# Hybrid trunk step (HGRN2, attention, Hyena, 16 experts): ring order of two modulation units, and an eighth place for expert weights in layer 1

## The reference

```python
a = jnp.einsum('td,edf->etf', t, w_gate)      # 16 experts, 1024 -> 512
b = jnp.einsum('td,edf->etf', t, w_up)
hid = jax.nn.silu(a) * b * gates.T[:, :, None]
out = jnp.einsum('etf,efd->td', hid, w_down)  # 512 -> 1024
```

## Time and profile before

| | |
|---|---|
| median of 3 runs | 874.86 us (872.3 to 875.55) |
| profiled execution | 872.13 us, its span 869.9 us |
| TensorE busy | 820.4 us, 94% |
| VectorE, ScalarE, GpSimd busy | 33%, 20%, 4% |
| DMA, mean | 336 GB/s over the span, 292.53 MB |
| expert stage of layer 0 | about 239 to 465 us |
| expert stage of layer 1 | about 633 to 861 us |

### The profile page before, as it was taken

One profiled execution on the slowest core, in us unless ns is written; L12 is line 12 of the kernel. 1 busy time (PEld: TensorE's weight loads), 2 busy tenths in 40 slices (PEclk: granted clock), 3 DMA queues, 4 the chain that ended last, 5 costly groups with the idle time before them and its releaser, 6 DMA issues.

```text
span 869.9 us, 13266 instructions
## 1 busy us (share of the span) xinstructions
PE 820.4 (94%) x5760; PEld 514.4 (59%) x5760; DVE 284.2 (33%) x587; ACT 176.4 (20%) x308; POOL 37.9 (4%) x67
## 2 busy tenths in 40 slices
PE   4999999799899999999999999999899999999997
PEld 3867778687643555345536888788643555345434
DVE  2155533614631211112114844662531212121113
ACT  4056013411511110111013212300411101110111
POOL 5000000030300000000000000000210000000000
PEclk8999999999999999999999999999899999999999
DMA  9999866652999999999999869255599999999981
GB/s 307 387 312 369 303 225 239 245 193 97 406 418 405 422 429 429 428 429 428 429 407 386 296 245 333 100 192 196 209 387 394 419 430 429 428 429 429 428 364 50
DMA packets 60004, 292.53 MB, mean 336 GB/s; under 512 B 2993, under 2 KB 5158, under 8 KB 47604
## 3 DMA queue, kind: packets, MB, share of 16 engines
q1 hardware_dynamic: 57940, 289.69, 83.5%
q10 hardware_dynamic: 1248, 1.08, 0.5%
q0 software_dynamic: 768, 1.04, 0.5%
HBM read 290.10 MB, written 1.70 MB: 335 GB/s over the span
## 4 chain that ended last, share of the span: by engine, by line
PE 70%; DMA 20%; DVE 7%; issue 1%; ACT 1%; SPq 1%; DVEq 0%
PE ps L1887 20%; DMA ring<-in_moe_w_up 17%; PE ps L1910 7%; PE ps L2018 6%; PE ps L1477 4%; PE ps L1541 4%; PE ps L1873 4%; PE ps L1663 3%; PE ps L1749 3%; PE ps L1535 3%; PE ps L1516 3%; PE ps L1923 2%; DMA ring<-in_mod_w 2%; PE ps L2014 1%; DVE hs L1117 1%
## 5 line engine op out<-in xcount | busy, mean ns | idle before, releaser
L1887 PE MATMUL ps<-ring,arena 128*64 128x512 f32 x896 | 224.7, 593 | 12.4 <-DMA ring<-in_moe_w_up 10.7
L1887 PEld LDWEIGHTS ps<-ring,arena 128*64 128x64 f32 x896 | 75.8, 137 | 118.6 <-issue 116.6
L1910 PE MATMUL ps<-ring,arena 128*64 128x512 f32 x512 | 113.4, 595 | 1.1 <-ACT arena L798 1.1
L1910 PEld LDWEIGHTS ps<-ring,arena 128*64 128x64 f32 x512 | 36.2, 137 | 66.4 <-issue 63.2
L1268 DVE SCALAR_TENSOR_TENSOR arena<-ps,arena 128x256 f32<-128x256 f32 x32 | 20.0, 668 | 163.0 <-PE ps L1887 163.0
L2018 PE MATMUL ps<-hs,ring 128*128 128x256 f32 x320 | 70.3, 380 | 0.0
L2018 PEld LDWEIGHTS ps<-hs,ring 128*128 128x128 f32 x320 | 60.5, 190 | 9.3 <-issue 1.4
L1873 PE MATMUL ps<-arena 128*128 (+1 forms) x512 | 60.0, 275 | 0.0
L1873 PEld LDWEIGHTS ps<-arena 128*128 128x128 f32 x512 | 58.4, 192 | 0.4 <-issue 0.4
L1887 PE MATMUL ps<-hs,arena 128*64 128x512 f32 x128 | 56.3, 593 | 0.0
L1477 PE MATMUL ps<-ring,csil 128*32 128x128 f32 x1536 | 51.2, 290 | 4.4 <-DVE arena L909 4.1
(11 more groups left out here) (310 smaller groups left out, 837.5 us busy)
## 6 DMA issues: line engine op xcount, KB each, us to landing
ring<-in_moe_w_up SPq DMA_DIRECT2D x32, 2048.0 KB, 17.2
ring<-in_moe_w_down SPq DMA_DIRECT2D x32, 2048.0 KB, 13.3
ring<-in_mod_w SPq DMA_DIRECT2D x24, 2048.0 KB, 12.7
ring<-in_moe_w_gate SPq DMA_DIRECT2D x24, 2048.0 KB, 13.9
hs<-in_moe_w_gate SPq DMA_DIRECT2D x8, 2048.0 KB, 17.4
ring<-in_hy_in_w SPq DMA_DIRECT2D x6, 2048.0 KB, 12.7
ring<-in_ab_in_w SPq DMA_DIRECT2D x4, 2048.0 KB, 13.1
ring<-in_ab_in_w SPq DMA_DIRECT2D x5, 1024.0 KB, 18.7
```

The lines of the kernel that those rows point to most:

```text
L1887: ins = mm(bank(4 + w)[e * 64:e * 64 + 64, :], xg[:, k, e * 64:e * 64 + 64], weights[:, k, :], start=(k == 0), stop=(k == KD - 1))
L1910: ins = mm(bank(6 + half)[e * 64:e * 64 + 64, :], hidT[:, f, e * 64:e * 64 + 64], down_unit(n + 4 + e)[:, f, half * 512:half * 512 + 512], ...
```

## The change

Modulation blocks 14 and 15 go into the list ahead of the two output units, and the small loads of the filter network are issued two places after `OUT0_AT` (which has moved by two), so one unit later in the list. In layer 1 another 16 KB per partition, `late_spare` (arena columns 11776 to 15872), become a place for the second expert's gate: even pairs have it there, odd pairs in the ring. It may be filled after the hyena's last FFT products (`t_y`). Both gates of a pair are then loaded a pair ahead: in layer 1 the order of pair `i` is gates of `i + 1`, ups and downs of `i` for `i` up to 3; for 4 ups, gates, downs; after that ups, downs, gates. Layer 0's order within the experts is unchanged. No product changes.

```diff
-UNITS += [("about", 0), ("about", 1)] + MODS[14:16]
+UNITS += MODS[14:16]
 OUT0_AT = len(UNITS)
+UNITS += [("about", 0), ("about", 1)]
...
-                    if n == OUT0_AT + 3:
+                    if n == OUT0_AT + 2:
...
+                def load_gate(i, j, dst):
+                    m = n + j
+                    sp.wait_ge(ring_free[m % RING], i + (m // RING - 1))
+                    arrived(sp, m, i - 1)
+                    load(i, j, dst)
...
+                else:
+                    sp.wait_ge(q["t_y"], 2)
+                    arrived(sp, n + 1 - RING)
+                    load(0, 1, late_spare)
+                    load_in_place(0, (0,))
+                    load_gate(1, 1, unit(n + 1))
+                    load_in_place(0, (2, 3, 4, 5))
+                    sp.wait_ge(q["t_htm"], 2 * l + 2)
+                    load_gate(1, 0, spare)
+                    for i in range(1, NPAIR):
+                        if i > 4:
+                            load_in_place(i, (2, 3, 4, 5))
+                        if i == 4:
+                            load_in_place(i, (2, 3))
+                        if i + 1 < NPAIR:
+                            load_gate(i + 1, 0, unit(n) if i % 2 else spare)
+                            load_gate(i + 1, 1, late_spare if i % 2 else unit(n + 1))
+                        if i == 4:
+                            load_in_place(i, (4, 5))
+                        if i < 4:
+                            load_in_place(i, (2, 3, 4, 5))
...
+                                elif w == 0 and e == 1 and l == 1 and not odd:
+                                    weights = late_spare
```

More of the change, by code:

```diff
@@ L311, in build @@
         Y3 = arena[:, 16256:17792].bitcast(BF16).rearrange("p (n c) -> p n c", n=3)
+        late_spare = arena[:, 11776:11776 + UNIT].rearrange("p (k c) -> p k c", k=KD)
         xg = M["xg"].rearrange("p (k c) -> p k c", k=KD)
@@ L481, in load_in_place @@
                         load(i, j, down_unit(m) if j >= 4 else unit(m))
[L483 to L496, removed]
+                def load_gate(i, j, dst):
[3 more added lines that the diff above has]
+                    load(i, j, dst)
+                if l == 0:
+                    load_in_place(0, range(6))
+                    sp.wait_ge(q["t_htm"], 2 * l + 2)
+                    load_gate(1, 0, spare)
+                    for i in range(1, NPAIR):
+                        load_in_place(i, (1,))
+                        if i + 1 < NPAIR:
[8 more added lines that the diff above has]
+                    load_in_place(0, (2, 3, 4, 5))
+                    sp.wait_ge(q["t_htm"], 2 * l + 2)
+                    load_gate(1, 0, spare)
+                    for i in range(1, NPAIR):
+                        if i > 4:
+                            load_in_place(i, (2, 3, 4, 5))
+                        if i == 4:
+                            load_in_place(i, (2, 3))
+                        if i + 1 < NPAIR:
+                            load_gate(i + 1, 0, unit(n) if i % 2 else spare)
+                            load_gate(i + 1, 1, late_spare if i % 2 else unit(n + 1))
+                        if i == 4:
+                            load_in_place(i, (4, 5))
+                        if i < 4:
+                            load_in_place(i, (2, 3, 4, 5))
                 n += 6 * NPAIR
@@ L1885, in gate_and_up @@
                             for e in range(2):
-                                weights = spare if odd and w == 0 and e == 0 else unit(n + 2 * w + e)
+                                weights = unit(n + 2 * w + e)
+                                if w == 0 and e == 0 and odd:
+                                    weights = spare
+                                elif w == 0 and e == 1 and l == 1 and not odd:
+                                    weights = late_spare
                                 ins = mm(bank(4 + w)[e * 64:e * 64 + 64, :], xg[:, k, e * 64:e * 64 + 64],
```

## The result

| | before | after |
|---|---|---|
| median of 6 runs | 873.24 us (871.88 to 875.55) | 865.31 us (862.99 to 868.51) |
| ratio, 95% interval | | 0.993 (0.9907 to 0.9953) |
| profiled execution, span | 872.13, 869.9 us | 864.91, 862.5 us |

The account below looks back on a forecast made before the run. TensorE waiting for up-projection transfers in the two expert stages was taken as what faster weights could gain, 10.7 us. Layer 1 -3.9 and layer 0 +0.8 sum to -3.1 us: 873.6 becomes 870.5 us, range 866.0 to 874.5.

Parts of the forecast that it names:

- The bound: Both expert stages: TensorE waits for up-projection transfers, 5.0 us in layer 0 and 5.7 in layer 1, 10.7 us in all.
- Part one, cover of the moved transfers: Output units issued some 7 and 11 us later still land 12 us or more before their products: no cost.
- Part one, cost of 0.8 us: Layer 0's expert stage: the queue runs empty as in layer 1, adding a fourth wait; 0.8 us lost, bounds 0 to 0.9.
- Part two, mechanism: Layer 1's eighth place stores one more unit, removing waits before pairs 4, 5 and 6; gain 3.9 us, bounds 2.8 to 5.7.
- The lag of the landing: Expert-stage queue: 1.7 us from issue to first byte, and 3.2 us from a unit's counted end to its landing.
- The wait before pair 3: Layer 1: pair 3's second up lands at 724.9 to 725.3, so the first wait stays, 0.8 to 1.2 us.
- The margin before pair 7's down half: Layer 1: pair 7's downs land at 846.6, needed at 846.8, so no wait there.
- the prediction's last sentence: Sign of error: layer 0's three waits shrink, or waits appear before a down half.
- No wait is left in layer 1, layer 0 as it was: Rival: a lag 1.7 us shorter removes all waits in layer 1; -5.7 us, 867.9 us, chance 0.15.
- The lead is spent: Rival: 1 us more at each of layer 1's three restarts brings waits back; -0.5 to +0.5, 873.6 us, chance 0.15.
- slower: Rival: waiting for the spare gate near 642 delays layer 1's restart past 647; 874.9 us or more, chance 0.07.
- Layer 0 gains too: Rival: earlier loads give layer 0 a lead of two units, removing its three waits (5.0 us); 864.7 us, chance 0.08.

Follow-up runs that it names:

- before_again: The kernel before the change, unchanged, traced a second time; first gate product to last down half 220.23 us in layer 0, 218.71 in layer 1.
- short_first_pair: Changed kernel, loading only an eighth of each of pair 0's four gate and up units in layer 0; layer 0's stretch 218.40 us (one execution).
- after_again: The changed kernel, unchanged, traced a second time; first gate product to last down half 218.69 us in layer 0, 213.24 in layer 1.
- place_only: Kernel before plus only layer 1's eighth place (`late_spare`) and its order, old list of units; 865.17 us, ratio 0.9921.
- both_orders: Kernel before plus layer 1's eighth place with its order, and in layer 0 late ups and downs passing gates (pairs 5, 6); 864.91 us, ratio 0.9916.
- after_both_orders: Changed kernel plus, in layer 0, ups of pair 5 and ups and downs of pair 6 ahead of the next pair's spare gate; 862.85 us, ratio 0.9889.
- gates_last: Changed kernel, but in layer 1 ups and downs of each pair go ahead of the next pair's gates from pair 1 on; 874.13 us, ratio 1.0024.
- mods_only: Kernel before with only modulation 14 and 15 moved ahead of the output units, no eighth place; 870.32 us, ratio 0.9996.
- half_downs: Changed kernel, loading only half of every down unit from pair 1 on in both layers; one execution, span 859.9 us.

## Why the prediction was right or wrong

**The bound** was read rightly: what moved in layer 1 are waits for transfers of its expert weights, four for ups before, one for an up and one for a down after. Between the last down half of layer 0 and the first gate product of layer 1 before and after take the same 175.85 us.

**Part one, cover of the moved transfers:** right. SP's issues in after (start, time from the first to the last issue of the row, line):

```profile
144.15 4.43 SPq L466 DMA_DIRECT2D ring<-in_ab_out_w  x2
...
183.23 11.61 SPq L478 DMA_DIRECT2D ring<-in_moe_w_gate  x2
203.96 11.06 SPq L478 DMA_DIRECT2D ring<-in_moe_w_up  x2
...
232.81 1.50 SPq L478 DMA_DIRECT2D hs<-in_moe_w_gate  x1
...
265.45 0.80 SPq L478 DMA_DIRECT2D ring<-in_moe_w_down  x2
...
640.28 0.33 SPq L478 DMA_DIRECT2D ring<-in_moe_w_gate  x1
...
659.88 0.81 SPq L478 DMA_DIRECT2D ring<-in_moe_w_down  x2
...
771.10 0.81 SPq L478 DMA_DIRECT2D ring<-in_moe_w_down  x2
```

The output units went out at 144.15 and some 4 us later, the gates of pair 0 at 183.23, the ups from 203.96, the spare gate at 232.81, 4.1 us ahead of the first gate product as before; it landed after 12.7 us, where 13 to 14 were forecast. No wait appeared in the output projection.

**Part one, cost of 0.8 us: wrong step.** The row came out as forecast (a fourth wait, 0.73 us), for a reason the runs don't bear out. I took layer 1's wait of 0.77 as the price of an empty queue and layer 0's zero as the price of a full one, each from one trace. `before_again` has 0.48 and 1.66 us there with the old order. The step that failed is reading a difference of 0.8 us between two stretches of one execution as an effect of the backlog; the waits of the first starved pairs differ by more than that between executions. The backlog did go, as forecast. GB/s in 40 slices of 0.4 us of after, 264:280, against the earlier trace rows:

```profile
GB/s 492 287 410 123 123 82 532 0 369 205 369 410 328 532 410 328 532 369 328 574 369 369 573 287 451 532 328 451 451 369 492 410 328 532 451 287 573 369 328 614
```

One slice is at 0 where before's lowest is 123. It isn't what sizes the wait: that follows the landing of pair 3's second up, which took 20.0 us from its issue in before, 20.8 in after, and 21.8 in `before_again`, which has the old order. Why the landing differs is open. That the term should be about zero rather than a gain was right, and `short_first_pair` shows the reason given for it, that the ring has no place, to be the right one.

**Part two, mechanism:** right in its main lines; sizes off. The gain was 5.5 us instead of 3.9. Two terms were mis-sized.
- The lag of the landing. The count put 1.7 us between an issue to an empty queue and its first byte, and 3.2 us between the counted end of a unit and its landing, 4.9 us in all, from one row of layer 1. In after the second up unit of pair 7, the twelfth behind the issue at 771.10, was issued at 812.7 and landed 20.4 us later, at 833.1: 62.0 us behind 771.10, which is 3.4 more than its twelve units of 4.89. With 1.5 us less the forecast wait before pair 7's up half, 1.7, becomes 0.2; it is 0.27. In `after_again` the lag is 3.8 us and the wait 0.75. Which of the two parts was too long, the rates tell. GB/s in 40 slices of 0.4 us, in 636:652, 655:671 and 768:784:

```profile
GB/s 451 369 451 451 369 164 82 82 0 0 0 0 0 532 41 246 287 492 246 451 492 287 532 451 287 573 369 369 573 328 410 532 287 492 532 287 492 492 287 553
...
GB/s 410 328 492 451 369 492 451 328 492 451 328 451 492 369 451 492 328 164 532 410 246 614 410 287 573 369 369 573 369 369 573 287 451 532 328 451 492 328 451 532
...
GB/s 451 532 287 492 492 205 164 41 41 0 451 82 164 328 410 369 451 410 369 492 287 492 532 287 492 533 287 492 532 287 492 532 287 492 532 287 451 573 287 451
```

The queue is empty from 639.2 in the first row, and runs down from 770.0 to nothing at 771.6 in the third; the issues stand at 640.28 and 771.10, and data flows at 641.2 and 772.0, both 0.9 us later. But the slices behind the first are thin, and the rate is full only some 2 us behind the issue. What moved in 771.10:830 of after, and in 661.33:690 of before:

```profile
DMA packets 1681, 24.61 MB, mean 418 GB/s; under 512 B 179, under 2 KB 179, under 8 KB 179
```

```profile
DMA packets 803, 11.63 MB, mean 406 GB/s; under 512 B 93, under 2 KB 93, under 8 KB 93
```

At 428 GB/s the 24.61 MB are 57.5 us of 58.9, the 11.63 MB 27.2 of 28.7. So counted in bytes the queue is 1.4 and 1.5 us behind one that runs in full from the issue, and the 1.7 us was nearly right. The part that was mis-sized is the 3.2 us of landing: about 2 in after. It was one reading of one unit, and it differs between traces as the waits do.
- The wait before pair 3. I let it stand at 0.8. It is absent in after, `after_again`, `place_only` and `short_first_pair`, 0.28 in `both_orders` and 0.79 in `after_both_orders`. As forecast, the queue doesn't run dry when the downs of 659.88 are due: the second row has one low slice, at 661.8. Again the landing came sooner than counted: pair 3's second up landed at 722.6, which is 724.1 with the 1.45 us by which this stage starts earlier than in before, where the forecast had 724.9 to 725.3 and TensorE is ready at 724.3. It is a margin of 0.2 us, and the scatter of the landings decides.

The margin before pair 7's down half, forecast at 0.2 us, went the other way: a wait of 1.05. Those two downs are the last large transfers and were issued at 826.08. The second landed 73.3 us behind 771.10, as forecast (73.4), but TensorE was ready 1.3 us sooner than counted, since the wait ahead of it had shrunk. By the prediction's last sentence a wait before a down half was a sign that it is wrong, and here the sign holds: part of what the shorter landing gives at the up half is taken back at the down half, which the prediction didn't name. Since ScalarE held the same product by 0.56 us before, it costs 0.5. The sum was 2.5 us of waits left; 1.3 was measured, 0.8 net of ScalarE's.

**The total.** Layer 1 explains 5.5 of the 7.4 us of span. The 2.2 us ahead of the first gate product aren't shown to belong to the change: that point lies at 239.12 and 238.85 in before, 236.92 and 238.19 in after, and 235.75 and 240.66 in two kernels whose program up to there is after's. 1.6 of the 2.2 us are a difference in granted clock that comes and goes in both kernels (last section). Taken out, the span would have fallen 5.2 us, and 873.6 less 5.2 is 868.4, well inside the range. The chance of 0.28 for faster by over 0.5% was too low: it rested on a forecast with two waits in layer 1, each of which was put at its long end. The two errors of the sum, 0.8 too much for part one and 1.6 too little for part two, point the same way and didn't cancel: they took the median to the edge of the range.

**The rivals.** "No wait is left in layer 1, layer 0 as it was" came closest, at -5.7 us. "The lead is spent" and "slower" have their place, in `gates_last`: the queue empties early and the lead is gone, ratio 1.0024. "Layer 0 gains too" is refuted by `mods_only` and `short_first_pair`.

**The skill's figures.** The HBM limit of about 358 GB/s (the Trainium skill, DMA: Bandwidth & Descriptors, Specifications) isn't seen in after either: 422 to 433 GB/s in most slices of both stages. The fixed 2.0 us (same page, Anatomy of one DMA) is a fit for GpSimd's path, and these transfers are SyncE's. The runs show something alike at a restart: the queue's last bytes ahead of the spare gate's landing at 640.2 flow until about 639.2, and new data comes 0.9 us after the issue, so 2.0 us of empty queue in all. But the lag of twelve units from issue to landing, 3.4 and 3.8 us, lies between the page's 2.0 and the count's 4.9; the estimate with 1.5 us less came nearer to the wait before pair 7 (0.2 against 0.27) than the count did, though not through the restart that it shortened.

## What to carry to other kernels

Where a stream of transfers is a little slower than its consumer, count the full places at the last moment the queue can run dry; transfers moved ahead of that moment give nothing without a place to put them. Then look at the order of the queue late in the stage: letting what is needed next pass what is needed a step later cashes the store once and needs no new memory; here it was worth about 2.5 us a stage. Done at the first pair it lost the gain. And before a wait of under 2 us in one trace becomes a term, look whether a second trace of the same program has it.

## What the runs showed of the hardware that was not expected

An empty queue takes up work again 0.9 us after an issue, but is at its full rate only some 2 us behind the issue: in bytes it is 1.4 to 1.5 us behind (after and before, above). The landing of a unit in a full queue isn't a fixed time behind its bytes. What moved in the 58.0 us behind the issue of pair 1's downs in layer 0, in before and in `before_again` (the same program):

```profile
DMA packets 1672, 24.25 MB, mean 418 GB/s; under 512 B 192, under 2 KB 192, under 8 KB 192
```

```profile
DMA packets 1652, 23.97 MB, mean 413 GB/s; under 512 B 189, under 2 KB 189, under 8 KB 189
```

At 428 GB/s the difference is 0.7 us. But pair 3's second up, the twelfth unit, landed 62.8 us behind that issue in before and 65.2 in `before_again`, 2.4 apart.

The first 240 us of this program differ by up to 4.9 us between executions of programs that are the same there. One part is TensorE's granted clock. A stretch in the recurrence's output of before, then the same work in after (busy us and instructions of PE, PEld, DVE, ACT, POOL, then granted clock, DMA share and GB/s):

```profile
156.60:164.60 8.00, 6.51 (x36) 4.63 (x36) 4.21 (x8) 3.44 (x5) 0.00 (x0) 0.79 0.87 318
```

```profile
156.00:164.00 8.00, 5.92 (x45) 4.17 (x46) 5.81 (x8) 5.01 (x6) 0.00 (x0) 1.00 0.98 360
```

In before the granted clock is 0.79 of 2.4 GHz on average there, so TensorE spent part of the stretch at the lower of its levels after a short idle time (1.16 us before the scores at 158.75); in after, with the same idle time ahead of the same products, it is 1.00. The scores took 2.08 us against 1.16 and the transposes behind them 2.64 against 1.96, and that is the 1.6 us by which the work behind them moved. It isn't the change: in 155:165 the clock is at 1.00 in `place_only`, at 0.83 in `after_again`, and at 0.66 in `half_downs`:

```profile
155.00:165.00 10.00, 7.24 (x56) 5.35 (x56) 6.25 (x8) 6.23 (x9) 0.00 (x0) 1.00 0.88 318
```

```profile
155.00:165.00 10.00, 7.37 (x43) 5.52 (x43) 5.53 (x8) 5.41 (x7) 0.00 (x0) 0.83 0.87 321
```

```profile
155.00:165.00 10.00, 8.09 (x36) 5.89 (x36) 4.63 (x8) 4.13 (x6) 0.00 (x0) 0.66 1.02 374
220.00:240.00 20.00, 17.97 (x223) 13.58 (x222) 13.51 (x40) 9.64 (x19) 7.32 (x8) 0.91 0.60 227
```

It is below 1.00 there in nine of the fourteen traces, with and without part one. In `half_downs` it falls a second time before the stage, a modulation product takes 3.50 us instead of 1.95, and both together make most of its late start. What decides it was not tried.
